# Fifty-four products of constants on TensorE behind the last product of a two-layer trunk

## The reference, cut to what matters

```python
for l in range(DEPTH):                       # 2 layers, x is 512 x 1024 float32
    h = rmsnorm(x, norm_mix[l])
    ...                                      # two attentions, gates, w_out
    x = x + mix @ w_out[l]
    h = rmsnorm(x, norm_ffn[l])
    x = x + hierarchical_moe(h, ...)         # top-1 of 8 groups, top-2 of its 8 experts
return rmsnorm(x, norm_final)
```

## Time and profile before

| what | value |
|---|---|
| median of 3 runs | 1911.36 us |
| lowest and highest run | 1909.36 and 1912.26 us |
| span of the profiled execution | 1909.3 us |
| its own time outside the span | not recorded separately |
| TensorE matmul busy | 1874.4 us, 98% |
| TensorE weight loads busy | 1571.5 us, 82% |
| VectorE busy | 1424.5 us, 75% |
| ScalarE busy | 1204.7 us, 63% |
| mean granted TensorE clock | 0.995 |

### The profile page before, as it was taken

The page is one execution under the profiler, slowest core; times in us unless marked ns, Lnnn a source line. Parts: engine busy times, 40 slices in busy tenths (PEclk is TensorE's granted clock), DMA queues, the critical chain, the costliest instruction groups (busy, mean ns, idle before and its releaser), DMA issues.

```text
span 1909.3 us, 26740 instructions
## 1 busy us (share of the span) xinstructions
PE 1874.4 (98%) x9252; PEld 1571.5 (82%) x9252; DVE 1424.5 (75%) x1776; ACT 1204.7 (63%) x1476; POOL 113.4 (6%) x169
## 2 busy tenths in 40 slices
PE   9999999999999999999999999999999999999997
PEld 7988878888888888888789788788888888888886
DVE  5465545589898899889835655454988998899897
ACT  5465544367777777777645555434677777777775
POOL 1000000130000000000000000002300000000000
PEclk9999999999999999999999999999999999999999
DMA  5221293499999999999432222825999999999992
GB/s 170 78 67 45 72 242 111 170 345 406 390 376 377 382 388 366 390 393 375 167 127 59 67 67 83 235 91 197 367 405 385 382 369 386 392 369 386 388 375 112
DMA packets 158793, 503.56 MB, mean 264 GB/s; under 512 B 22410, under 2 KB 38794, under 8 KB 158704
## 3 DMA queue, kind: packets, MB, share of 16 engines
q1 hardware_dynamic: 146192, 459.70, 64.3%
q0 software_dynamic: 12512, 42.69, 7.4%
HBM read 490.18 MB, written 32.79 MB: 274 GB/s over the span
## 4 chain that ended last, share of the span: by engine, by line
PE 91%; DVE 5%; issue 2%; ACT 1%; DMA 1%; DVEq 0%; SPq 0%; POOL 0%; ACTq 0%; POOLq 0%
PE ps L1682 26%; PE ps L1684 26%; PE ps L1683 26%; PE ps L1928 3%; PE ps L1863 2%; PE ps L1912 2%; PE ps L2060 1%; DVE wl L1148 1%; PE ps L2019 1%; PE ps L1973 1%; DMA yb<-yrows 1%; PE ps L2031 1%; PE ps L1729 1%; DVE gb L1440 1%; DVE ml L1203 1%
## 5 line engine op out<-in xcount | busy, mean ns | idle before, releaser
L1148 DVE TENSOR_TENSOR wl<-raw,wh 128x2048 fp32r<-128x2048 f32 (+1 forms) x402 | 901.1, 2277 | 162.5 <-ACT wh L750 161.2
L750 ACT ACTIVATE wh<-raw 128x2048 fp32r<-128x2048 f32 (+1 forms) x406 | 745.7, 1884 | 63.7 <-PE ps L1684 63.7
L1682 PE MATMUL ps<-wh,xgh 128*128 128x512 f32 x1024 | 405.7, 396 | 0.3 <-DVE wl L1148 0.3
L1684 PE MATMUL ps<-wh,xgl 128*128 128x512 f32 x1024 | 399.3, 390 | 0.0
L1683 PE MATMUL ps<-wl,xgh 128*128 128x512 f32 x1024 | 399.2, 390 | 0.0
L1684 PEld LDWEIGHTS ps<-wh,xgl 128*128 128x128 f32 x1024 | 192.3, 188 | 41.1
L1682 PEld LDWEIGHTS ps<-wh,xgh 128*128 128x128 f32 x1024 | 192.4, 188 | 39.0 <-DVE wl L1148 1.2
L1683 PEld LDWEIGHTS ps<-wl,xgh 128*128 128x128 f32 x1024 | 192.6, 188 | 37.8
L1682 PE MATMUL ps<-wh,hth 128*128 128x512 f32 x512 | 200.0, 391 | 1.9 <-DVE wl L1148 1.8
L1684 PE MATMUL ps<-wh,htl 128*128 128x512 f32 x512 | 199.7, 390 | 0.0
L1683 PE MATMUL ps<-wl,hth 128*128 128x512 f32 x512 | 199.3, 389 | 0.0
(11 more groups left out here) (320 smaller groups left out, 2572.2 us busy)
## 6 DMA issues: line engine op xcount, KB each, us to landing
raw<-in_w SPq DMA_DIRECT2D x512, 512.0 KB, 6.3
raw<-in_w SPq DMA_DIRECT2D x128, 1024.0 KB
raw<-in_w_gate SPq DMA_DIRECT2D x16, 1024.0 KB
xslots<-zrow POOLq DMA_DIRECT2D x2, 6240.0 KB, 35.6
raw<-in_w_out SPq DMA_DIRECT2D x8, 1024.0 KB
xg<-xslots POOLq DMA_DIRECT2D x14, 520.0 KB, 7.3
raw<-in_w_in SPq DMA_DIRECT2D x8, 800.0 KB
raw<-in_w_oa SPq DMA_DIRECT2D x4, 1024.0 KB
```

What stands on the lines that cost most here:

```text
L750: return nc.scalar.activation(dst, src, ACT.Copy)
L1148: return V.tensor_tensor(dst, src, hi.bitcast(F32), ALU.subtract)
L1682: MM(dst, lh, rh, start=first, stop=False)
L1684: return MM(dst, ll, rh, start=False, stop=last)
```

## The change

Behind `chained_blocks`, and so behind `overflow`, TensorE's stream gets one wait on `fin_sem["sq"]` and eight calls of a new function. It multiplies a constant by itself. `width` is how many of the array's columns hold weights, `cols` how many columns are streamed, `count` how many products there are. Successive products go to successive parts of the array's columns (PSUM partitions `c` to `c + width`) until `tiles_` of them are used, and then to the other of two banks. With the last argument 1 they all stay at the first columns and only the bank changes. Nothing reads the results. In all there are 54 products: 4 of fp32r, and 50 of fp32. Of those in fp32, 32 use 64 columns of the array (4 of these stay at the first 64), 8 use 32 columns, and 10 use all 128.

```diff
@@ -2116,6 +2116,26 @@
 
                 chained_blocks(pe, pe_block, y_settled, y_product)
 
+            pe.wait_ge(fin_sem["sq"], 1)
+            free = (ps[0], ps[4])
+
+            def column_tiles(weights, width, cols, count, wait_tiles=None):
+                tiles_ = wait_tiles or P // width
+                moving = weights[:, :].rearrange("p (o q) -> p o q", o=1).to_broadcast([P, 4, P])
+                for i in range(count):
+                    c = i % tiles_ * width
+                    rhs = moving[:, 0:cols // P, :] if cols >= P else weights[:, 0:cols]
+                    MM(free[i // tiles_ % 2][c:c + width, 0:cols], weights[:, c:c + width], rhs, start=True, stop=True)
+
+            column_tiles(upper_r, 64, 512, 4, 1)
+            column_tiles(ident, 64, 512, 8)
+            column_tiles(ident, 64, 256, 8)
+            column_tiles(ident, 64, 64, 12)
+            column_tiles(ident, 128, 64, 6)
+            column_tiles(ident, 32, 512, 8)
+            column_tiles(ident, 64, 256, 4, 1)
+            column_tiles(ident, 128, 256, 4)
+
 
```

## The result

The changed kernel takes 1920.89 us (median of 4 runs, 1918.12 to 1922.19) against 1911.81 for the kernel before (4 runs, 1909.36 to 1913.71). The ratio is 1.0044, with a 95% interval of 1.0028 to 1.0060: slower by 0.44%, 9.1 us by the medians. The profiled execution took 1920.35 us with a span of 1918.5, so 1.85 us lie outside the span.

What follows compares the result with a forecast made beforehand. TensorE bounds the kernel, VectorE's rows and then the stores its end. Span 1901.0 + 16.2 (products) + 0.95 (width changes) + 1.7 (clock) + 0.39 (end) = 1920.3, 11.0 later; on the median 1911.36 that gives 1922.4 us, range 1918 to 1936.

Steps and rivals of the forecast that it cites:

- The place of the added work: On TensorE behind the loop of `overflow`, in place of the drain: starts at 1901.0, not 1898.5.
- The cover: At the kernel's end, TensorE's idle time up to SyncE's drain at 1909.1: 8.1 us to hide added products under.
- not slower: Rival, at the kernel's end: TensorE's products are hidden and the time stays at 1911.4 us; chance 0.04.
- The fall of the clock: At the added work's start: clock at half rate for some 3.4 us, 1.7 us lost.
- The changes of width that were priced: Between the eight calls: five changes of array width at 0.19 us each, 0.95 us.
- The 3.3 us that the range kept for the fetch of added code: TensorE's 208 added instructions: fetching their code might cost up to 3.3 us; not counted, kept for the range.
- side by side: Likeliest case, added products in different columns: two records under way at any time, sum 16.2 us; chance 0.55.
- one after the other: Rival, added products: the array runs them singly whatever their columns; sum 25.5, time 1931.6 us; chance 0.30.
- the term of 3.44 us: Sixth call, 8 products of 32 by 512: 8 x 0.43 = 3.44 us, 1.72 if four went at once.
- The term of the short products: Fourth call, 12 products of 64 by 64, 24 records: 2.0 us, the middle between 2.69 and 1.34.
- The prediction's remark that 2.38 would put halves where the sum has them or lower: Added halves and quarters: the skill's 2.38 for three parts, scaled, would price them as the sum or somewhat lower.
- The clock stays low: Rival, second to seventh call: narrow products don't restore the clock, half rate adds 13.6 us; 1934.3 us; chance 0.11.

Runs made afterwards that it cites:

- the single call: The changed kernel with only the second call kept (8 products of 64 by 512), the other seven left out; 1911.79 us, ratio 0.9997 to the kernel before.
- two experiments: Against the changed kernel: places in the order a, a, b, b (1920.37 us); three calls in place of the eight, with 4 or 12 products in a row per place (1923.49 us).
- a third: Against the changed kernel: other calls, ten products in turn, then quarters and halves with three products in a row for each place; 1919.39 us in one run.
- in one place: The changed kernel with the halves and quarters of the second, third, fourth and sixth call all sent to the first columns; 1931.95 us, ratio 1.0106 to the kernel before.
- runs of a place: Three calls in place of the changed kernel's eight, with 4 or 12 products in a row for each place; 1923.49 us in one run.
- the doubled kernel: The changed kernel with twice as many products in every call; 1933.72 us, ratio 1.0115 to the kernel before.

## Why the prediction was right, and where it wasn't

The forecast of 1922.4 us (1918 to 1936) was met at 1920.89, and slower was right. The growth was 9.1 us for a forecast of 11.0. The main steps stand. The place of the added work was read rightly from the sequencer's rows: it starts behind the loop's branches, not behind the last product, and moving it ahead of the loop changes the time. The cover is what SyncE's stores leave, as the single call shows, and TensorE's drain sets the end, so the rival "not slower" falls. The fall of the clock came as forecast, 3.4 us long, and was worth 1.7 us: the first two calls took 6.18 for 6.25, and 4.5 (1900.82 to 1905.33) where they stand ahead of the loop and the clock doesn't fall. The changes of width that were priced cost 0.14 and 0.20 for 0.19. The 3.3 us that the range kept for the fetch of added code didn't show.

The choice between side by side and one after the other was the large one. It was decided by a mechanism that gave the right price for halves and the wrong one for quarters. The step that failed reads: "The next product's first record goes to other columns and may stream beside the second. Then two records are under way at any time, in halves and in quarters alike". First records of different products start together, with no wait for the second of the one before, and quarters go four at a time: the term of 3.44 us measured 1.72 (16 records in four rounds of 0.43). For halves the price came out right by luck of the count: with two places, two records are under way by either mechanism. The rule in its place is one running and one waiting product for each place, found in two experiments and forecast rightly in a third. The term of the short products was mis-sized: the 2.0 us were the middle between bounds of 1.34 and 2.69, and it took 24 x 0.058 / 2 = 0.70, below both. The lower bound was worked out with a half-price load but took no account of two loads at once, which the trace shows (20 loads in 0.66 us). These two errors make 3.0 of the 3.2 us by which the calls were too dear. Both were allowed for by the range, which named four quarters at once and cheap short products at its lower end. In the spans they were offset in part by the later start (1.4 us), of which 1.0 is difference between executions and the rest the longer branch; so a part of the closeness is luck.

"One after the other" is refuted for products in different places: in one place that pattern costs 11.1 us more (1931.95). The rival's time of 1931.6 is near that of this experiment, though its sum had 2.69 us for the short products, which take 24 x 0.058 = 1.4. The Trainium skill's page "TensorE: Matmul & The Clock Gate", section "Part 3: Packing small matmuls — row/col tiling", holds that a load passes a running matmul only if their row groups differ (and, in another sentence of the section, if it goes to a second, background buffer for weights). This trace disagrees with the first: in the sixth call eight loads of parts that share all rows fall within 0.16 us at 1912.54, beside the matmuls of the first four. The same section's 2.38 times for three parts has no counterpart here, as no run uses three; two parts went twice and four parts four times as fast within their calls (6.88 us one after the other, 3.43 and 1.72 so). The prediction's remark that 2.38 would put halves where the sum has them or lower was also misread: scaled to two parts it is under 1.6 times, a higher price than the sum's.

"The clock stays low" is refuted: in every trace with a fall the clock came back, under products on half the columns. It then stayed at 1.00 for 15.8 us of halves and quarters alone (runs of a place, 1905.6 to 1921.4), for 10.8 us of halves in one place (1907.0 to 1917.8), and for 24.6 us of all forms together in the doubled kernel.

## What to carry to other kernels

Narrow fp32 products in different halves or quarters of the columns, or halves of the rows, cost together what one of them costs, if they stand next to each other in the program and no third one for the same place comes before the others. A change of width costs 0.14 us (to half the columns) or 0.20 (to all of them), so a single narrow product between wide ones gains nothing. To price work at the end of an engine's stream, look where its sequencer is, not where its array is: here 3.25 us lay between, spent in the loop's branches. They brought a fall of the clock worth 1.7 us, and moving the work ahead of the loop hid only a part of them. Work that ended before the last store landed was free here, and what reached beyond it was paid (12.8 us measured for 13.3 added).

## What the runs showed of the hardware that wasn't expected

- A column place takes one running and one waiting fp32 product; a third blocks those for other places behind it. A product for a free place starts ahead of an earlier one that waits.
- A weight load costs by its columns: 0.112 us for 128, 0.058 for 64, and two loads for different halves share 0.058.
- When TensorE's sequencer reached the drain, or the loop behind the moved products, the array was at the first of the last 8 products (3.7 to 3.9 us of work) in the kernel with the change, with a single place, moved ahead and doubled. In runs of a place 8 products hadn't started and two were running.
- The first branch of a loop past the block took 3.3 to 3.9 us on TensorE at the end of every trace, on either side of the added products; the second and third took 0.22.
